# First block of a three-block model: sixteen panels of the input linear and two column pairs of the mixer's output linear by seven products instead of eight

## The reference

```python
proj = x @ w_in                       # 1024 -> 5632 columns (+ 16 step sizes, a small extra product)
z, xbc, dt_raw = ...                  # gate, convolved part, step sizes of the SSD mixer
sc_b, sc_c, sc_h = ...                # short convolution: three parts of 1024
xbc = silu(causal_dwconv(xbc, conv_w) + conv_b)
y_ssd = ssd_mixer(...)                # 16 heads: decay matrices exp(a_cs_l - a_cs_s), masked C.B, states; times silu(z); norm
y_sc = sc_b * causal_dwconv(sc_c * sc_h, sc_conv_w)
mix = concatenate([y_ssd, y_sc]) @ w_out          # 2048 -> 1024
x = layer_norm(ALPHA * x + mix, ...)
```

## Time and profile before

| what | before |
| --- | --- |
| median of 3 runs | 2311.67 us |
| profiled execution | 2312.58 us, span 2310.7 us |
| PE busy | 2213.1 us (96%) |
| PEld, DVE, ACT, POOL busy | 1514.3, 923.1, 382.4, 435.2 us |
| mean granted TensorE clock | 0.995 |

### The profile page before, as it was taken

One profiled execution on the slowest core, in us unless ns is written; L12 is line 12 of the kernel. 1 busy time (PEld: TensorE's weight loads), 2 busy tenths in 40 slices (PEclk: granted clock), 3 DMA queues, 4 the chain that ended last, 5 costly groups with the idle time before them and its releaser, 6 DMA issues. The chain is left out here.

```text
span 2310.7 us, 35107 instructions
## 1 busy us (share of the span) xinstructions
PE 2213.1 (96%) x14557; PEld 1514.3 (66%) x14557; DVE 923.1 (40%) x1961; ACT 382.4 (17%) x857; POOL 435.2 (19%) x365
## 2 busy tenths in 40 slices
PE   8999999999999998998999999999999999989998
PEld 7888899987799987887633333333333333358887
DVE  4242465744444564626333333333333333243322
ACT  2210130124201023225200000000000000023331
POOL 0120498820088851012000000000000000000000
PEclk9999999999999999999999999999999999999999
DMA  7334654464864454323699999999999999962422
GB/s 265 127 126 146 240 167 159 168 223 181 318 221 170 158 186 159 128 111 138 249 416 428 428 427 429 428 427 428 406 426 427 429 427 427 428 269 100 165 76 89
DMA packets 61155, 619.36 MB, mean 268 GB/s; under 512 B 6800, under 2 KB 8080, under 8 KB 12304
## 3 DMA queue, kind: packets, MB, share of 16 engines
q1 hardware_dynamic: 59328, 611.08, 66.5%
q10 hardware_dynamic: 1712, 6.63, 0.8%
HBM read 616.63 MB, written 1.05 MB: 267 GB/s over the span
## 5 line engine op out<-in xcount | busy, mean ns | idle before, releaser
L2958 PE MATMUL ps<-expert_ring,moe_xg 128*64 128x512 f32 x1280 | 281.8, 593 | 10.0 <-DMA expert_ring<-we_dram 9.8
L3004 PE MATMUL ps<-expert_ring,mix_y 128*64 128x512 f32 x1024 | 228.7, 596 | 11.8 <-DMA expert_ring<-we_dram 11.8
L2958 PEld LDWEIGHTS ps<-expert_ring,moe_xg 128*64 128x64 f32 x1280 | 90.5, 137 | 190.0 <-issue 167.5
L466 PE MATMUL ps<-x_res,ring 128*128 128x256 f32 x896 | 201.3, 383 | 8.5 <-DMA x_res<-x_dram 8.5
L466 PEld LDWEIGHTS ps<-x_res,ring 128*128 128x128 f32 x896 | 169.7, 192 | 33.0 <-DMA ring<-w_in_dram 8.5
L3270 DVE TENSOR_SCALAR mix_y<-ps 128x512 f32<-128x512 f32 x32 | 22.1, 692 | 421.6 <-PE ps L2958 421.6
L2775 POOL COPY unscaled_x<-modulations 128x8 f32<-128x8 f32 x1 | 0.2, 198 | 937.2 <-POOLq L3059 937.2
L2958 PE MATMUL ps<-ring,moe_xg 128*64 128x512 f32 x768 | 168.2, 593 | 0.5 <-DVE moe_xg L2919 0.3
L3004 PEld LDWEIGHTS ps<-expert_ring,mix_y 128*64 128x64 f32 x1024 | 69.8, 137 | 148.4 <-issue 126.6
L466 PE MATMUL ps<-third_h,ring 128*128 128x256 f32 x704 | 158.0, 380 | 0.0
L625 POOL TENSOR_TENSOR seven_weights<-ring 128x512 f32<-128x512 f32 (+1 forms) x72 | 94.1, 1307 | 325.5 <-DVE seven_x_turned L641 288.8
(11 more groups left out here) (624 smaller groups left out, 3311.2 us busy)
## 6 DMA issues: line engine op xcount, KB each, us to landing
expert_ring<-we_dram SPq DMA_DIRECT2D x144, 2048.0 KB, 23.1
ring<-we_dram SPq DMA_DIRECT2D x47, 2048.0 KB, 25.7
ring<-w_in_dram SPq DMA_DIRECT2D x55, 1024.0 KB, 4.9
ring<-ffn_up_dram SPq DMA_DIRECT2D x44, 1024.0 KB, 5.0
ring<-ada_dram SPq DMA_DIRECT2D x36, 1024.0 KB, 4.8
ring<-w_out_dram SPq DMA_DIRECT2D x16, 1024.0 KB, 5.0
ring<-ffn_dn_dram SPq DMA_DIRECT2D x16, 1024.0 KB, 5.0
ring<-ple_g_dram SPq DMA_DIRECT2D x8, 1024.0 KB, 6.8
```

The source lines that it names most:

```text
L466: mm = pe.matmul(core.ps[:, bank_of[n, c], 0:TOK], w[:, k * PANEL + c * P:k * PANEL + c * P + P], sources[panel](k0 + k), start=(k0 + k == ...
L2958: mm = pe.matmul(ps[out, bank, :], xg[:, j % 4, j // 4, :], w[:, bank * D + at:bank * D + at + 512], start=False, stop=(j == 7))
L3004: mm = pe.matmul(ps[out, 2, :], hidt[:, at_k:at_k + S], w[:, i * D + at:i * D + at + 512], start=False, stop=(k == DT - 1))
```

## The change

`w_in` pairs 6 to 21 (one panel each) and `w_out` pairs 1 and 2 (two panels each, with `keep` for the first of them) become fast. `takes` learns a set of pairs (`only`). POOL itself makes the four activation sums of `x` for `w_in` at the start (`turn_input`). The sums for `w_out` are made by DVE in section 43 (`turn_mixed`). POOL's heads get one section each, beginning with section 20, and so stand two by two behind the panel sums of pairs 10 to 17. The LayerNorm takes the factor ALPHA out of the tiles whose first panel `keep` has already scaled.

```diff
     def takes(self, name, j):
-        return name in self.first_pair and j >= self.first_pair[name]
+        return name in self.first_pair and j >= self.first_pair[name] and (name not in self.only or j in self.only[name])
...
     def gpsimd(pool):
+        for _ in range(FIRST + 1):
+            yield
         pool.wait_ge(cbm_ready.sem, cbm_ready.at(1))
         pool.wait_ge(silu_done.sem, silu_done.at(3))
         for h in range(SSD_HEADS):
...
             pool.tensor_tensor(wl[:, h % 2, TOK:TOK + P], ex[:, h % 2, TOK:TOK + P],
                                xbc[:, 10 + g, P:TOK], ALU.mult).then_inc(w_ready.sem, 1)
-        yield
+            yield
...
-            if m < 6 and self.alpha != 1.0 and not self.split:
+            if m < 6 and self.alpha != 1.0 and not self.split and m // 2 not in self.kept:
                 return e.scalar_tensor_tensor(out=x, in0=x, scalar=self.alpha, in1=p, op0=ALU.mult, op1=ALU.add)
...
+FAST_IN, FAST_OUT = tuple(range(6, 22)), (1, 2)
...
+        parts_fast |= {"w_in": (FAST_IN[0], turned_x, None, groups("w_in"), FAST_IN),
+                       "w_out": (FAST_OUT[0], turned_y, norms[0].keep, groups("w_out"), FAST_OUT)}
...
+        def turn_input(pool):
+            clear(pool)
+            pool.wait_ge(core.sem_f.sem, core.sem_f.at(16))
+            seven.turn(pool, seven.groups["w_in", 0], core.x[:, 0:4, :], core.x[:, 4:8, :], *(x_turned[:, i, :, :] for i in (0, 2, 1, 3)))
+
+        def turn_mixed(dve):
+            yield WOUT0 - 1
+            for t in range(WOUT0 - DT, WOUT0):
+                core.wait_tile(dve, t)
+            seven.turn(dve, seven.groups["w_out", 0], y_sc[:, 0:4, :], y_sc[:, 4:8, :], *(out_turned[:, 0, i, :, :] for i in (0, 2, 1, 3)))
+            xd_ready(dve, DT - 1)
+            seven.turn(dve, seven.groups["w_out", DT], xd[:, 0:4, :], xd[:, 4:8, :], *(out_turned[:, 1, i, :, :] for i in (0, 2, 1, 3)))
...
-        linear(core, parts, None, tiles, head=head, act_work=more_loads, pool_work=clear, banks=3,
+        linear(core, parts, None, tiles, head=head, act_work=more_loads, pool_work=turn_input, banks=3,
```

More of the change, by code:

```diff
@@ L575, in __init__ @@
         self.first_pair, self.moving_of, self.keepers = {}, {}, {}
-        for name, (first, moving, keeper, groups) in parts.items():
+        self.only = {}
+        for name, (first, moving, keeper, groups, *only) in parts.items():
             self.first_pair[name], self.moving_of[name], self.keepers[name] = first, moving, keeper
+            if only:
+                self.only[name] = only[0]
             for k0, n in groups.items():
@@ L630, in sums, with turn @@
         pool.tensor_tensor(s4, a12, s2, ALU.subtract).then_inc(summed.sem, 1)
-    def turn(self, dve, n, upper, lower, t1, t2, t3, t4):
+    def turn(self, eng, n, upper, lower, t1, t2, t3, t4):
         turned = self.turned
         b11, b12, b21, b22 = upper[:, :, 0:P], upper[:, :, P:TOK], lower[:, :, 0:P], lower[:, :, P:TOK]
[L636 to L641, removed]
+        eng.tensor_tensor(t1, b12, b11, ALU.subtract).then_inc(turned.sem, 1)
+        eng.tensor_tensor(t3, b22, b12, ALU.subtract).then_inc(turned.sem, 1)
+        eng.wait_ge(turned.sem, turned.at(4 * n + 1))
+        eng.tensor_tensor(t2, b22, t1, ALU.subtract).then_inc(turned.sem, 1)
+        eng.wait_ge(turned.sem, turned.at(4 * n + 3))
+        eng.tensor_tensor(t4, b21, t2, ALU.subtract).then_inc(turned.sem, 1)
     def copy_first(self, act, n, one):
@@ L1125, with __init__ @@
 class LayerNorm:
-    def __init__(self, core, run, n, g, b, first, alpha, split, fill):
+    def __init__(self, core, run, n, g, b, first, alpha, split, fill, kept=()):
         self.core, self.run, self.n, self.first, self.alpha, self.fill = core, run, n, first, alpha, fill
@@ L1133, in __init__ @@
         self.sem = dict(zip(names, (*core.shared[28:40], *core.shared[61:63])))
-        self.split = split
+        self.split, self.kept = split, kept
         self.added_before = 0
@@ L1727, in first_block @@
         norms = [LayerNorm(core, run, n, (lambda k, l=l, g=g: core.v(g, l * DT + k)), (lambda k, l=l, b=b: core.v(b, l * DT + k)), first,
-                           alpha, split, mods.fill)
+                           alpha, split, mods.fill, FAST_OUT if first == WOUT0 else ())
                  for n, (g, b, l, first, alpha, split) in enumerate((
@@ L1795, in turned_h, with turned_y @@
             return h_turned[:, {5: 0, 6: 1, 4: 2}[product], k0 // 2 + p, :]
-        turn_order = [("ffn_up0", 0), *(("ffn_dn0", k0) for k0 in range(0, FF_T, KG)), ("ple_g0", 0),
+        out_turned = h_turned[:, :, :, :].rearrange("p c w n -> p (c w n)")[:, 0:2 * 4 * (DT // 2) * P].rearrange(
+            "p (g c w n) -> p g c w n", g=2, c=4, n=P)
+        def turned_y(product, k0, p):
+            return out_turned[:, k0 // DT, {5: 0, 7: 1, 6: 2, 4: 3}[product], p, :]
+        turn_order = [("w_in", 0), ("w_out", 0), ("w_out", DT), ("ffn_up0", 0), *(("ffn_dn0", k0) for k0 in range(0, FF_T, KG)), ("ple_g0", 0),
                       ("ffn_up1", 0), *(("ffn_dn1", k0) for k0 in range(0, FF_T, KG)), ("ple_g1", 0)]
@@ L1821, in turn_h @@
             return program
-        turns = [turn_x("ffn_up0", UP0, norms[0]), turn_h("ffn_dn0", UP0), turn_x("ple_g0", PG0, norms[1]),
+        turns = [turn_mixed, turn_x("ffn_up0", UP0, norms[0]), turn_h("ffn_dn0", UP0), turn_x("ple_g0", PG0, norms[1]),
                  turn_x("ffn_up1", UP1, norms[2]), turn_h("ffn_dn1", UP1), turn_x("ple_g1", PG1, norms[3])]
```

## The result

The changed kernel takes 2340.3 us (median of 4 runs, 2334.3 to 2341.8) against 2312.1 for the kernel before on the same chip (4 runs, 2311.3 to 2314.5: the three of the table before and one more): ratio 1.0112, 95% interval 1.0101 to 1.0124. It is slower by 28 us; 2338 was predicted. The profiled execution, whose rows follow, took 2334.3 us with a span of 2332.2; it was the fastest of the four.

A forecast was written before the change was run, and what follows sets the result against it. PE, busy 96% of the span, was taken to bound the kernel. -13.2 + 1.4 + 29.1 + 3.0 + 4.3 + 0.7 + 1.7 = +27.0 us gave 2338.7 from the runs' median; predicted 2338, range 2328 to 2348.

The forecast's parts named there:

- Panels: Sixteen w_in and four w_out panels become fast, 6.25 us each against 6.91: 13.2 us less.
- Sections 18 and 19: Back to back behind a fast panel, section 19 waits for DVE's copy of the chunk states: 1.4 us stall.
- The loop: Pairs 10 to 18: end of panel, POOL's head, weight sums, next panel form a closed loop; PE waits 29.1 us.
- contention: In the loop, 15 DVE instructions meet POOL's chain and slow it by about 0.2 us each: 3.0 us.
- the clock: Four waits after pairs 14 to 17 are each followed by half clock, 1.07 us lost each: 4.3 us.
- d: Time from PE's panel end to POOL's head start: 2.4 us (pairs 10 to 13; 2.1 at 10), 4.0 (14 to 17).
- The clock stays up: Rival: no clock falls behind the loop's waits, since PE works again at once; 2334 us, chance 0.18.
- Falls in all eight: Rival: the clock falls in every one of the eight waits and stays down into the sections; 2348 us, chance 0.12.
- Tile 43: End of w_in: DVE's reciprocal in section 41 delays tile 43, which PE wants for its eighth matmul: 0.7 us stall.
- L1169: Behind pair 24, sections 48 and 49 back to back: L1169 waits for combine_rest, tile 48 and its addition, 1.7 us.
- The delay passes to the end: Behind the LayerNorm nothing changes and PE's progress releases later loads, so the whole +27.0 us reaches the kernel's end.
- POOL hides it all: Rival: POOL's 7.5 us a pair fits within PE's 8.28 if heads start before the panel ends; 2302 us, chance 0.07.

The follow-up runs named there:

- the waits filled: The changed kernel with 7 (pairs 11 to 14) or 14 (pairs 15 to 18) extra 128x128x128 matmuls on PE before product 5: 2335.9 us, ratio 1.0099.
- made true by one section: The changed kernel with POOL's heads begun one section later (FIRST + 2 for FIRST + 1): 2311.0 us, ratio 0.9986 against the kernel before.
- the segment first: The changed kernel with DVE's convolution of a sc_h tile put behind the head's segment of the same section: 2331.9 us, ratio 1.0086 against the kernel before.
- plain head pairs: The changed kernel with w_in pairs 11 to 18 ordinary again: 2311.0 us, ratio 0.9987 against the kernel before.

## Why the prediction was right

Direction, size and mechanism came out as predicted, 2340.3 for 2338 (the sum gave 2338.7; the text gives no reason for the 0.7 it drops). By its own steps:

- *Panels, −13.2 us.* In w_in, too, fast panels that nothing holds follow at 6.25 us (204.36 to 210.61). With 0.66 us each the balance closes: −16 × 0.66 + 1.36 + 34.7 = +25.5 for 25.3 measured at w_out.
- *Sections 18 and 19, 1.4.* Measured 1.36. The convolutions of the early pairs cost nothing, as taken: PE had no other wait there.
- *The loop, 29.1, with contention 3.0 and the clock 4.3:* together 36.4, measured 34.7, of which 2.6 are contention and 3.3 the clock (below), so that 28.8 are left for the loop. Its pieces: d was put at 2.4 and 4.0; POOL's head started 106.83 − 104.40 = 2.43 and 143.11 − 139.22 = 3.89 us behind the section. The wait before product 5 was put at about 2 and 3.5; it was 2.0 and 3.7. The periods without the clock were put at 11.0 and 12.6, and with 0.2 us for each meeting of DVE and POOL 11.2 and 13.2; measured 11.24, and 13.08 with the waits filled. The case from which the 7.46 us was read, the first fast panel of another layer, was the right one.
- *Contention.* None after pair 10, 0.17 us after each of pairs 11 to 13 (L628 1.44 in place of 1.27) and about 0.5 after each of pairs 14 to 17 (L1113 0.64 for 0.46, L628 1.44, L631 1.45, or L629 in the last): 2.6 us for the 3.0 taken, in 15 lengthened instructions as counted. The Trainium skill (SBUF — State Buffer, section "SBUF: two separate sides") has each engine lock the pair of ports for a whole instruction. The 15 meetings came, but each cost POOL under 0.2 us and not the up to 0.42 that this would allow. What the sum did not price is the other side, DVE's own slowing: under the loop it was free, as the prediction said of it, and it became the bound as soon as the loop was gone.
- *The clock, 4.3.* 3.3 us in the profiled run, by the window with the waits filled: four falls behind the long waits, as put, but at 0.56 each (13.64 − 13.08) and not 1.07, and one (1.1 us) behind a wait of 2.03 us, which had been put at none. Its other three waits of 2.02 to 2.19 us had none. So the total is near by two errors that offset each other, a small piece of luck. "The clock stays up" is refuted. "Falls in all eight" is refuted for the two profiled executions; these were the shortest of their four, and the six others, at a mean clock of 0.991 to 0.992, may have had more falls, though none came near the 2348 us of that rival.
- *Tile 43, 0.7, and L1169, 1.7.* Measured 0.42 and 1.56.
- *The end of w_out to the end.* "The delay passes to the end" is where the text was lucky: this execution kept 21.5 of its 25.2 us, and the medians differ by 28.2. Between profiles clock falls at later stalls and the wait for a load near 591 us come and go, up to 2 us each; the range had to hold that, and did.

The rival "POOL hides it all" had the totals right (POOL is busy 62%) and the order wrong; when its condition was made true by one section, the result was 2311, not its 2302, mostly since DVE beside POOL then held the heads.

## What to carry to other kernels

Where engines run in a fixed order, follow one round of the new work from engine to engine and look for an instruction that waits on the end of the last round and has the start of the next one queued behind it: an engine that is 62% busy can cost more than it saves, and one section's shift in its order can take that back. Price a loop by a case of the same chain elsewhere in the trace. Then ask what the wait was hiding: here an overlap of DVE and POOL that makes some of DVE's instructions 2.4 to 4 times as long, so that the new work pays only in pairs where DVE has little to do.

## What the runs showed of the hardware that was not expected

- DVE slows beside a busy POOL also where it reads one SBUF tensor and a column: L804 from 0.35 to 1.24 and 1.36 us. L809, with two tensors, goes from 0.5 to 1.4 each, while POOL's own sum grows only from 1.27 to 1.45. The loss is far from even: DVE pays a factor of 2.4 to 4, POOL 1.15.
- The clock's answer to a stall isn't fixed. Of four waits of 2.02 to 2.19 us in the profiled run after one was followed by a fall, of four of 3.67 to 3.69 all; with the segment first, a wait of 2.20 ending at 99.02 us had a fall (2.07 us for product 5) and four of 2.21 to 2.23 had none at once. The stall of 2.38 us had a fall before, and after it none.
- With PE kept busy through the waits the clock stayed at 1.00, and the eight periods got 3.3 us shorter although PE did 84 matmuls more in them. Over the whole kernel the gain isn't clear of the spread. (The Trainium skill, TensorE: Matmul & The Clock Gate, section "Part 1: The HAM clock gate", has an idle engine fall to the lower clock; the filled waits, with no fall, agree.)

Open: how much of the spread between runs is clock falls (shown by correlation alone), and how often the part won in the first block is given back later, as in the run with plain head pairs. The waits of 1.4 us at section 19 and 0.4 at tile 43 were left as they are.
